# Part of a conditioning product moved from TensorE to GpSimd, and a modulate stage that loads all its inputs at once

## What is computed

```python
sh1, sc1, g1, sh2, sc2, g2 = split(silu(c) @ ada_w + ada_b, 6)   # ada_w: 1024 x 6144
csh1, csc1, ... = split(silu(c_ctx) @ ada_w + ada_b, 6)
h_ctx = rmsnorm(ctx, norm1_g) * (1 + csc1) + csh1
h     = rmsnorm(x, norm1_g) * (1 + sc1) + sh1
proj  = h @ w_in                       # columns: conv A, conv B, q, i, ff, fb, g, 512 each
u     = proj_A * sigmoid(proj_B)
conv  = silu(layernorm(dwconv_grid(u, 31 taps) + bias))
```

## Time and profile before

| | us |
|---|---|
| median of 3 runs (2538.88 to 2545.4) | 2539.48 |
| the profiled execution's own time | 2538.86 |
| its span in the profile | 2537.0 |
| TensorE busy | 2269.9 (89%) |
| VectorE busy | 1555.3 (61%) |
| ScalarE busy | 1038.6 (41%) |
| GpSimd busy | 524.8 (21%) |
| last VectorE instruction of the modulate stage ends | 173.95 |
| first projection matmul of the conv stage starts | 186.13 |
| first mean matmul of the conv stage's layer norm starts | 503.75 |

### The profile page before, as it was taken

The page is one execution under the profiler, slowest core; times in us unless marked ns, Lnnn a source line. Parts: engine busy times, 40 slices in busy tenths (PEclk is TensorE's granted clock), DMA queues, the critical chain, the costliest instruction groups (busy, mean ns, idle before and its releaser), DMA issues. The chain is left out here.

```text
span 2537.0 us, 38841 instructions
## 1 busy us (share of the span) xinstructions
PE 2269.9 (89%) x14873; PEld 1538.4 (61%) x15020; DVE 1555.3 (61%) x2214; ACT 1038.6 (41%) x1329; POOL 524.8 (21%) x554
## 2 busy tenths in 40 slices
PE   6779999999598899876998289999999999999996
PEld 2334444444397878763554177777777777777773
DVE  1644999743366877853333646666666666666666
ACT  1321101145356565553444134444444444444445
POOL 0010000100354554632333301111111111111111
PEclk9889999999799999978999589999999999999998
DMA  7544101222301111005443366667777666767676
GB/s 257 189 137 95 34 17 30 87 55 75 112 9 47 53 38 52 22 25 197 157 154 117 124 229 225 222 224 229 232 232 232 224 222 223 225 231 231 223 248 250
DMA packets 217155, 379.54 MB, mean 150 GB/s; under 512 B 43469, under 2 KB 72781, under 8 KB 216537
## 3 DMA queue, kind: packets, MB, share of 16 engines
q1 hardware_dynamic: 200168, 320.86, 37.7%
q0 software_dynamic: 16896, 57.52, 8.4%
HBM read 314.62 MB, written 63.72 MB: 149 GB/s over the span
## 5 line engine op out<-in xcount | busy, mean ns | idle before, releaser
L89 PE MATMUL pgu<-xhi,mwhi 128*128 128x256 bf16 x2048 | 559.0, 273 | 0.8 <-DVE xlo L2065 0.8
L90 PE MATMUL pgu<-xlo,mwhi 128*128 128x256 bf16 x2048 | 559.1, 273 | 0.0
L91 PE MATMUL pgu<-xhi,mwlo 128*128 128x256 bf16 x2048 | 559.0, 273 | 0.0
L2070 DVE TENSOR_TENSOR mwlo<-mwst,mwhi 128x2048 bf16<-128x2048 f32 x187 | 426.8, 2283 | 0.0
L1974 ACT ACTIVATE mwhi<-mwst 128x2048 bf16<-128x2048 f32 x186 | 350.8, 1902 | 0.0
L1982 ACT ACTIVATE thb<-pgu 128x256 f32<-128x256 f32 x128 | 49.1, 384 | 549.8 <-PE pgu L91 549.8
L547 DVE SCALAR_TENSOR_TENSOR co<-u,taps,co 128x1984 f32<-128x1984 f32 (+22 forms) x120 | 234.1, 1951 | 3.7
L89 PEld LDWEIGHTS pgu<-xhi,mwhi 128*128 128x128 bf16 x2048 | 200.6, 98 | 25.8 <-DVE xlo L2065 1.1
L90 PEld LDWEIGHTS pgu<-xlo,mwhi 128*128 128x128 bf16 x2048 | 200.6, 98 | 24.6
L91 PEld LDWEIGHTS pgu<-xhi,mwlo 128*128 128x128 bf16 x2048 | 200.7, 98 | 23.6
L1914 POOL TENSOR_TENSOR mpflag<-mpflag 1x1 f32<-1x1 f32 x46 | 37.1, 806 | 854.5 <-DVE ysb L2097 579.1
(11 more groups left out here) (296 smaller groups left out, 4361.8 us busy)
## 6 DMA issues: line engine op xcount, KB each, us to landing
mwst<-in_w_gate SPq DMA_DIRECT2D x32, 2048.0 KB, 9.2
mwst<-in_w_up SPq DMA_DIRECT2D x32, 2048.0 KB, 7.9
mwst<-in_w_down SPq DMA_DIRECT2D x32, 2048.0 KB, 10.8
ada<-in_ada_w SPq DMA_DIRECT2D x12, 2048.0 KB
wst<-in_w_in SPq DMA_DIRECT2D x20, 512.0 KB, 5.0
s_rows<-row SPq DMA_DIRECT2D x16, 520.0 KB, 2.8
xb<-in_x SPq DMA_DIRECT2D x4, 2048.0 KB, 13.1
mx<-s_mixed SPq DMA_DIRECT2D x16, 512.0 KB, 3.9
```

Source lines behind the costliest of these rows:

```text
L89: nc.tensor.matmul(out, lh, rh, start=(k == 0), stop=False)
L90: nc.tensor.matmul(out, lh, rl, start=False, stop=False)
L91: last = nc.tensor.matmul(out, ll, rh, start=False, stop=(k == n - 1))
L2070: nc.vector.tensor_tensor(wlo[:, b, ks], wst[:, b % NS, ks], whi[:, b, ks], ALU.subtract)\
```

## The change

In **modulate_stage** only parts 0 to 3 are made, and each has its own buffer (`big`), so that SyncE issues all loads at once: the four parts, the context, and x groups 1 to 4, of which groups 2 to 4 go into the buffers that parts 0 to 2 leave. `ada_b` for them comes in one load into `modrow`. The first four slabs of w_in are loaded behind them, by the modulate stage (the new class `ConvWeights` holds the buffers `wst` over both stages). ScalarE squares groups 0 to 2 ahead of the loop, VectorE scales groups 0 and 1 ahead of it. `hf` has four buffers. Three of four low parts are made by GpSimd (`lo`), the fourth by VectorE; before VectorE writes a buffer of `hf` again it waits for the low part that read it (`lod_ok`, `lop_ok`). GpSimd stores nothing here, and norm2_g is not used here.

In **conv_stage** GpSimd makes parts 4 to 11, each in two halves of 256 columns: it loads the half (`load_ada`), multiplies the 8 x 256 columns by silu(c) of their rows, adds 8 blocks to 4, to 2, to 1, and writes `msum`. The loads use the memory of `sq`, `rs`, `y` and `tl` (`late`), so ScalarE waits for the last half before the layer norm. TensorE adds over partitions with one fp32 matmul against a column of 0.5 and adds the bias with another, as eight jobs of the kind "mod" behind the projections 5, 6, 8, 9, 10, 12, 13 and 15. The stores of all jobs are issued by ScalarE. Behind the projections are then 20 jobs; 17 follow them as before, but they begin with the same v job.

In **outproj_stage** VectorE makes (1 + sc2) * norm2_g once, which the modulate stage made before, and norm2_g is loaded there.

```diff
-def modulate_stage(nc, K, I, scr):
-    NCH = 12
+def modulate_stage(nc, K, I, scr, CW_):
+    NCH = 4
...
-        ada = m.sb("ada", [P, 2, KD, SEG])
-        xb = m.sb("xb", [P, 2, 4, D])
-        hf = m.sb("hf", [P, 2, SEG])
+        big = m.sb("big", [P, NCH, KD, SEG])
+        xc = m.sb("xc", [P, 2, D])
+        x1 = m.sb("xg1", [P, 4, D])
+        hf = m.sb("hf", [P, 4, SEG])
...
+        def on_dve(q):
+            return q % 4 == 3
...
+        def lo(engine, q):
+            g, k = divmod(q, KD)
+            t0, n = groups[g]
+            engine.tensor_tensor(K["hlo"][:, k, t0 * P:(t0 + n) * P], hf[:, q % 4, 0:n * P],
+                                 K["hhi"][:, k, t0 * P:(t0 + n) * P], ALU.subtract)\
+                .then_inc(lod_ok if on_dve(q) else lop_ok, 1)
...
-                load_ada(0)
-                load_ada(1)
-                load_x(0)
-                load_x(1)
-                load_ada(2)
-                load_ada(3)
+                for n in range(NCH):
+                    sp.dma_start(big[:, n], ada_v[:, :, n * SEG:(n + 1) * SEG]).then_inc(ada_in[n], 16)
...
+                for g, (t0, n) in enumerate(groups):
                     src = I["ctx"][0] if g == 0 else I["x"][0, (t0 - 2) * P:(t0 - 2 + n) * P, :]
                     if g >= 2:
+                        sp.wait_ge(mod_ps, g - 1)
+                    sp.dma_start(rows_of(g), src.rearrange("(n p) d -> p n d", p=P)).then_inc(x_in[g], 16)
+                for s in range(4):
+                    CW_.load(sp, s)
...
+                for q in range(NQ):
+                    if not on_dve(q):
+                        pool.wait_ge(hf_ok, q + 1)
+                        lo(nc.gpsimd, q)
...
-                        for c in chunks_with(g)[2 * k // KD:2 * k // KD + 1]:
-                            first = 2 * k % KD
-                            mod_mm(c, range(first, first + 2))
...
+    MOD_AFTER = [5, 6, 8, 9, 10, 12, 13, 15]
+    for q in range(NCT * NSEG):
+        start = len(KIND)
+        if q >= NSEG:
+            KIND.append(("v", q - NSEG))
+        if q in MOD_AFTER:
+            KIND.append(("mod", MOD_AFTER.index(q)))
+        AFTER_U.append(range(start, len(KIND)))
...
+        ada = late[:].rearrange("p a b j -> p (a b j)").rearrange("p (s k e) -> p s k e", s=2, k=KD)
+        msum = m.sb("msum", [P, 3, SEG])
...
+                for e in range(2 * NMOD):
+                    n, h = divmod(e, 2)
+                    a = ada[:, h]
+                    pool.wait_ge(ada_in[h], 16 * (n + 1))
+                    nc.gpsimd.tensor_tensor(a, a, K["csil"][:, 0, :].unsqueeze(2).broadcast_to([P, KD, EH]), ALU.mult)\
+                        .then_inc(ada_ok, 1)
+                    pool.wait_ge(ada_ok, 4 * e + 1)
+                    nc.gpsimd.tensor_tensor(a[:, 0:4], a[:, 0:4], a[:, 4:8], ALU.add).then_inc(ada_ok, 1)
+                    pool.wait_ge(ada_ok, 4 * e + 2)
+                    nc.gpsimd.tensor_tensor(a[:, 0:2], a[:, 0:2], a[:, 2:4], ALU.add).then_inc(ada_ok, 1)
+                    pool.wait_ge(ada_ok, 4 * e + 3)
+                    if h == 0 and n >= 3:
+                        pool.wait_ge(job_ps, mod_job[n - 3] + 1)
+                    nc.gpsimd.tensor_tensor(msum[:, n % 3, h * EH:(h + 1) * EH], a[:, 0], a[:, 1], ALU.add)\
+                        .then_inc(ada_ok, 1)
+                    if e + 2 < 2 * NMOD:
+                        load_ada(e + 2)
...
+                    act.wait_ge(job_ok, j + 1)
+                    act.dma_start(dst, src).then_inc(job_out[j % 2], 16)
...
+                act.wait_ge(ada_ok, 8 * NMOD)
...
+                    elif what == "mod":
+                        pe.wait_ge(half_ok, 1)
+                        pe.wait_ge(adab_in, 16)
+                        pe.wait_ge(ada_ok, 8 * (r + 1))
+                        nc.tensor.matmul(bank[0:1, :], half[:, 0:1], msum[:, r % 3], start=True, stop=False)
+                        last = nc.tensor.matmul(bank[0:1, :], K["ident"][0:NMOD, r:r + 1], adab[:], start=False, stop=True)
...
+                wait(dve, r_in, 80)
+                nc.vector.scalar_tensor_tensor(mrow[:, 1], mrow[:, 1], 1.0, n2r[:], ALU.add, ALU.mult).then_inc(sc_ok, 1)
```

More of the change, by code:

```diff
@@ L196, in square @@
                                              scale=1.0 / D).then_inc(std_ok, 1)
-                for j in range(groups[0][1]):
-                    square(0, j)
+                for g in range(3):
+                    for j in range(groups[g][1]):
+                        square(g, j)
+                act.wait_ge(a1_ok, 1)
                 for g, (t0, n) in enumerate(groups):
-                    if g == 0:
-                        act.wait_ge(a1_ok, 1)
                     s = 0 if g else 1
@@ L208, in _ @@
                                              bias=modc[:, k, s:s + 1], scale=A1[:, k, s:s + 1]).then_inc(hi_ok, 1)
-                        if k < 4 and g + 1 < len(groups):
-                            square(g + 1, k)
+                        if k >= KD - 4 and 1 <= g < len(groups) - 2:
+                            square(g + 2, k - (KD - 4))
             @block.vector
@@ L355, in conv_stage @@
         lg = m.sb("lg", [P, 2, NCT])
-        sq = m.sb("sq", [P, 2, SEG])
-        rs = m.sb("rs", [P, 2, SEG])
-        y = m.sb("y", [P, 2, SEG])
-        tl = m.sb("tl", [P, 2, SEG])
+        late = m.sb("late", [P, 4, 2, SEG])
+        sq, rs, y, tl = (late[:, i] for i in range(4))
+        ada = late[:].rearrange("p a b j -> p (a b j)").rearrange("p (s k e) -> p s k e", s=2, k=KD)
+        msum = m.sb("msum", [P, 3, SEG])
+        adab = m.sb("adab", [NMOD, SEG])
+        half = m.sb("half", [P, 1])
         mh = m.sb("mh", [P, 2, SEG], BF16)
@@ L375, in conv_stage @@
         m_out = m.sems("m_out", 2)
-        wv = I["w_in"][0].rearrange("(k p) n -> p k n", p=P)
+        EH = SEG // 2
+        ada_v = I["ada_w"][0].rearrange("(p k) e -> p k e", k=KD)
+        mod_job = [j for j in range(JOBS) if KIND[j][0] == "mod"]
         def ln_job(n, j):
@@ L383, in _ @@
             def _(sp):
-                for s, (col, _) in enumerate(SLAB):
-                    if s >= 4:
-                        sp.wait_ge(w_lo, s - 3)
-                    sp.dma_start(wst[:, s % 4], wv[:, :, col:col + P]).then_inc(w_in[s % 4], 16)
+                for s in range(4, len(SLAB)):
+                    sp.wait_ge(w_lo, s - 3)
+                    CW_.load(sp, s)
                 for n in range(NSEG):
@@ L418, in _, with load_ada @@
-                for i in range(2):
-                    pool.wait_ge(job_out[i], 16 * (JOBS // 2))
+                def load_ada(e):
+                    n, h = divmod(e, 2)
+                    c0 = (4 + n) * SEG + h * EH
+                    if e >= 2:
+                        pool.wait_ge(ada_ok, 4 * (e - 1))
+                    pool.dma_start(ada[:, h], ada_v[:, :, c0:c0 + EH]).then_inc(ada_in[h], 16)
+                nc.gpsimd.memset(half[:], 0.5).then_inc(half_ok, 1)
+                load_ada(0)
@@ L450, in _ @@
                             w_split(4 + n)
-                        else:
-                            job(q - NSEG)
+                        for j in AFTER_U[q]:
+                            job(j)
                     if c < 2:
@@ L501, in _ @@
                     job(j)
+                for i in range(2):
+                    act.wait_ge(job_out[i], 16 * (JOBS // 2))
             @block.vector
@@ L625, in _ @@
                         last.then_inc(ab_ps, 1)
-                        if c >= 1:
-                            job(q - NSEG)
+                        for j in AFTER_U[q]:
+                            job(j)
                 for j in range(WITH_U, WITH_U + WITH_TAPS):
@@ L2269, in build @@
             K["hlo"] = mm.sb("hlo", [P, KD, TC + T], BF16)
-            modulate_stage(nc, K, I, scr)
-            conv_stage(nc, K, I, scr)
+            K["csil"] = mm.sb("csil", [P, 2, KD])
+            with nc.cleanup_on_exit(), ExitStack() as front:
+                CW_ = ConvWeights(Mem(nc, front), I)
+                modulate_stage(nc, K, I, scr, CW_)
+                conv_stage(nc, K, I, scr, CW_)
             heads_stage(nc, K, I, scr)
```

224 lines of the change are left out of this document (110 added, 114 removed).

## The result

| | before | after |
|---|---|---|
| median of 6 runs each, us | 2540.77 (2538.88 to 2545.4) | 2552.26 (2550.09 to 2552.96) |
| after / before, 95% interval | | 1.0041 (1.0028 to 1.0053) |
| span of the profiled execution | 2537.0 | 2549.3 |
| first projection matmul | 186.13 | 106.08 |
| first mean matmul | 503.75 | 516.98 |

The change makes the kernel slower by 11.5 us, where 28 was forecast. The sign and the mechanism are those of the prediction; the size is less than half. The first projection comes 80.1 us sooner, and from there to the mean it takes 93.3 us longer.

What follows compares the result with a forecast made beforehand. The prediction took TensorE to bound the conv stage, VectorE close behind and stopped by GpSimd's sums after the change. Terms −76.4 + 103 + 3 − 1.5 = plus 28 on 2538.9 gave 2567 us, range 2535 to 2604, likeliest case 2550 to 2590.

Steps and rivals of the forecast that it cites:

- the mechanism: Conv stage: each GpSimd tensor_tensor stops VectorE's two-SBUF-input taps for its length, 7.2 us per half part.
- first projection: Modulate stage up to the first projection matmul: moves from 186.1 to 109.7, minus 76.4 us (bounds 66 and 84).
- projection to mean: Conv stage from first projection to first mean: 420.5 us against 317.6 now, plus 103.
- layer norm: ScalarE's store issues lengthen the layer norm's chain by 0.7 us a segment, plus 3 in all (bounds 0 and 8).
- change of stages: After the conv stage the last store lands sooner: minus 1.5 us.
- all later stages: Outproj stage's one more VectorE instruction (1.3 us) and load lie in VectorE's wait for TensorE: 0.
- the other 13.6 · 7.2 = 98 us fall on the taps: Conv stage: GpSimd does 2.4 halves before the taps start; the other 13.6 delay them 7.2 us each.
- the taps' start: Conv stage: VectorE starts the taps at 50 us or so after the first projection (48.3 before the change).
- Case D: Whole kernel: the two large terms cancel (front at best bound, hold 15% shorter), about 2542 us; chance 0.07.
- A: Conv stage rival: GpSimd doesn't stop the taps, TensorE bounds the stage, whole change -59 us, 2480; chance 0.11.
- B: Conv stage rival: GpSimd slower than rows of other shapes say, 10.6 us per half, 29 more, 2596; chance 0.12.
- C: Modulate stage rival: loads at half the rate bind the front, groups 3 and 4 wait, 2579 us; chance 0.06.

Runs made afterwards that it cites:

- e2: Changed kernel with each of GpSimd's 64 tensor_tensor instructions replaced by a memset of the same output, parts 4 to 11 not computed: 2474.0 us, ratio 0.9735.
- e6: Kernel before, with modulation parts 4 to 11 left out of its modulate stage and their rows filled from parts 0 to 3: 2498.8 us, ratio 0.9838.
- e4: Changed kernel with all 40 low parts of the modulate stage on VectorE, none on GpSimd: 2567.0 us, ratio 1.0101.
- e9: Changed kernel with the first four weight slabs loaded at the conv stage's start instead of the modulate stage's end: 2554.4 us, ratio 1.0058.
- e5: Changed kernel with the stores of the last 38 jobs issued by GpSimd again, ScalarE keeping the first 20: 2551.8 us, ratio 1.0044.
- e1: Changed kernel without GpSimd's 64 tensor_tensor instructions, one small memset per half part instead, loads kept, parts 4 to 11 not computed: 2476.0 us, ratio 0.9740.
- b4: Changed kernel with parts 4 to 7 on GpSimd, 8 to 11 on TensorE, and conv constants awaited only before the first tap: 2506.7 us, ratio 0.9871.
- e3: Changed kernel with each of GpSimd's 64 tensor_tensor instructions replaced by a tensor_scalar reading one operand, parts 4 to 11 not computed: 2518.9 us, ratio 0.9909.

## Why the prediction was right or wrong

In the profiled executions, forecast against measured:

| term | forecast | measured |
|---|---|---|
| first projection | -76.4 | -80.1 |
| projection to mean | +103 | +93.3 |
| layer norm | +3 | +2.6 |
| change of stages | -1.5 | -4.7 |
| all later stages | 0 | +1.2 |
| sum | +28 | +12.3 |

**The mechanism was right, and one term of the sum was mis-sized most: "the other 13.6 · 7.2 = 98 us fall on the taps".** That each GpSimd instruction stops VectorE held; its price did not. It measured 13 · 6.4 = 82.9, 15 less. Three parts of it: the 2048-column multiply takes 3.60 us and not 4.08, the half part 7.94 instead of 8.5 (13 · 0.56 = 7 us); what remains, 1.56 us of each half, is hidden at meetings, not 1.3 (3.4 us); and 13 halves met the taps, not 13.6 (4.3 us). The 4.08 came from the one row of 2048 columns, whose output and one operand are bf16. The prediction also weighed 4497 ns for fp32 of 2048 from the Trainium skill (GPSIMD Engine Reference, "Elementwise"); with a broadcast operand the trace has 3.60 us, so that figure pointed the wrong way here.

**Inside the stage** the taps' start was too early in the forecast: 54.8 us after the first projection, not 50, since the hold falls on the low weight parts too: the three right before the first tap take 9.98 us, and 3.50 in e2, where the taps start 48.6 us after the projection. I counted it on the taps alone. From u number 11 to the mean it was 158.1 us against 157.4. So the stage's term is 15 us less for the hold, 5 more for its start and 1 more behind it: 93.3 instead of 103.

**The front** was 3.7 us better than the sum: 1.2 of them already at A1 (51.6 against 52.8), the rest in the five groups. Runs e6, e4 and e9 give the parts of the gain, which the prediction had not separated.

**The change of stages** gained 4.7 us, of which e5 shows 1.9 to be the stores.

All terms but the last err on the same side, and together they are 16 us. The forecast was a difference of two terms near 80 and 100, so errors of 5 and 9% on the two took 13 us from a result of 28. Case D of the prediction said just this, at 0.07 and with 2542 (its own terms, 84 for the front and 14.7 off the hold, give 2545). The wide range, 2535 to 2604, held the time, but the likeliest case's own, 2550 to 2590, held it only at its lower edge, with the terms off as above. The change is slower by 0.41%, more than the 0.3% that the prediction called measurable, but the interval reaches down to 0.28%.

**The rivals.** A (taps not stopped, 2480) is what e1 and e2 show without the sums' reads: 2476 and 2474. Its sum was right to 4 and 6 us; its condition was false in the changed kernel. B (slower GpSimd) was false with the opposite sign. C (loads bind) was false: TensorE waits in the front for no load after its first part's, and ScalarE for an x group's only 1.2 us.

**The signs named beforehand**: single taps of 5 to 6 us behind the 2048-column instruction (5.74), the mean of the group up (2.58, forecast 2.8), waits for u in seven projections (65.0 us, forecast 80), none for the sums, and taps at their old length after GpSimd's end. These came. The first projection "near 110" came at 106.1, and the mean "near 530" at 517.0, 13 us too early.

## What to carry to other kernels

Idle time of GpSimd is not free beside VectorE instructions that read two SBUF tensors: price its tensor_tensor at its own length on VectorE's chain, and look for an engine whose idle time falls at another place, or for a split of the work over two. Where a forecast is the difference of two large terms, the sign may hold while the size does not: measure the price of the exact instruction shape before trusting the sum. A local gain ahead of a stage bound by another engine (late slabs: 4.6 us, of which 0.7 arrived) must not be carried to the end; and a wait for constants belongs before the instruction that reads them (b4, 6 us at the mean).

## What the hardware showed beside that

**VectorE's instructions with one SBUF input are held too, in some forms.** The prediction took only those with two. Groups of VectorE in the changed kernel, norms of 60 to 105 us and the first tap (a tensor_scalar) of the four channel tiles:

```profile
L233 DVE TENSOR_SCALAR big<-big,rstd 128x1024 f32<-128x1024 f32 x12 | 10.7, 895 | 0.1
...
L578 DVE TENSOR_SCALAR co<-u,taps,cb 128x2048 f32<-128x2048 f32 x4 | 9.0, 2262 | 0.0
```

The first stands at 749 ns when GpSimd has no low parts (e4). The second's mean hides one instruction; here are the four (ns min/median/max), which take 1343 ns in the mean in e2:

```profile
L578 DVE TENSOR_SCALAR co<-u,taps,cb x4: 1341/1542/4620, 160.9 to 438.3; 128x2048 f32<-128x2048 f32 x4
```

The one of 4.62 us (at 281.28) has GpSimd's 2048-column multiply beside it. Together the four add 3.7 us, part of the 82.9. So both forms are held by GpSimd's tensor_tensor. Whether its reads or its writes do it is not shown for them: no memset of e2 stands beside one of the four. In e3 it went the other way once: the one at 254.71 kept its 1.34 us, and GpSimd's tensor_scalar beside it took 3.73 instead of 2.77. In b4 a tensor_scalar of 124 columns took 3.63 us beside GpSimd, and 0.23 in the changed kernel. The form with an accumulator and the instructions that read PSUM with one SBUF operand (u, 679 ns against 682 in e2) kept their times. The Trainium skill (SBUF — State Buffer, "Who interferes with whom") says that copy, cast and tensor_scalar, but not the form that writes its accumulator, can contend with GpSimd; the rows agree for tensor_scalar and for the form with an accumulator, and show no copy or cast.

- GpSimd's memset of 2048 fp32 columns took 1.82 us and held no tap; its tensor_scalar took 5.4 to 5.6 us, half as long again as the tensor_tensor with a broadcast operand (3.60), and overlapped with the tap's own work for at least some 1.9 us.
- 16 MB of loads into SBUF, issued by GpSimd, added nothing to the taps (234.2 against 234.1 us).
- GpSimd's queue paused 12 to 15 us behind its first four to six small loads in the conv stage, in either order.
